# One attention phase: maxima taken in pairs, low parts of weight units one step behind, the convolution's split one group later

## The reference, cut to what matters

```python
proj = n @ w_in[l]
y_conv = short_conv_mixer(b_gate, c_gate, h_conv, conv_w[l], w_conv_out[l])
...
def short_conv_mixer(b_gate, c_gate, h_in, conv_w, w_out):
    u = c_gate * h_in
    up = jnp.pad(u, ((0, 0), (CONV_WIDTH - 1, 0), (0, 0)))
    conv = sum(up[:, k:k + S, :] * conv_w[k] for k in range(CONV_WIDTH))
    return (b_gate * conv) @ w_out
...
s = jnp.where(mask, s.astype(jnp.float32), -jnp.inf)
m = jnp.max(s, axis=-1, keepdims=True)
e = jnp.exp(s - m)
return e / jnp.maximum(jnp.sum(e, axis=-1, keepdims=True), 1e-30)
...
mix = jax.nn.sigmoid(g_conv) * y_conv + jax.nn.sigmoid(g_attn) * y_attn
h = h + mix @ w_o[l]
```

## Time and profile before

| | us |
|---|---|
| median of 3 runs | 761.01 (760.69 to 763.24) |
| the profiled execution | 764.64 |
| its span | 762.9 |
| TensorE busy | 752.9 |
| VectorE busy | 519.9 |
| ScalarE busy | 421.4 |

### The profile page before, as it was taken

The page is one execution under the profiler, slowest core; times in us unless marked ns, Lnnn a source line. Parts: engine busy times, 40 slices in busy tenths (PEclk is TensorE's granted clock), DMA queues, the critical chain, the costliest instruction groups (busy, mean ns, idle before and its releaser), DMA issues.

```text
span 762.9 us, 12541 instructions
## 1 busy us (share of the span) xinstructions
PE 752.9 (99%) x5015; PEld 668.0 (88%) x5015; DVE 519.9 (68%) x848; ACT 421.4 (55%) x808; POOL 71.0 (9%) x111
## 2 busy tenths in 40 slices
PE   9999999999999999999999999999999999999998
PEld 8999988798899988888888888999888888888886
DVE  4884676777574767888357766889568777447762
ACT  5484556457364447566345555697636665445640
POOL 6300000001011000250000003500100000000000
PEclk9999999999999999999999999999999999999999
DMA  7998454235334556665655562754453655655611
GB/s 238 307 310 276 77 124 141 99 111 166 111 112 172 172 181 194 196 214 187 218 181 192 169 217 59 231 157 141 163 166 122 210 200 188 218 168 170 210 63 56
DMA packets 108430, 131.33 MB, mean 172 GB/s; under 512 B 5357, under 2 KB 97595, under 8 KB 108372
## 3 DMA queue, kind: packets, MB, share of 16 engines
q1 hardware_dynamic: 105780, 125.58, 50.9%
q0 software_dynamic: 2304, 4.43, 2.6%
q10 hardware_dynamic: 288, 0.52, 0.2%
HBM read 128.68 MB, written 1.84 MB: 171 GB/s over the span
## 4 chain that ended last, share of the span: by engine, by line
PE 85%; DVE 9%; ACT 3%; issue 2%; DMA 0%; SPq 0%; ACTq 0%; DVEq 0%
PE B L1552 27%; PE B L1529 21%; PE B L1513 16%; PE B L1534 11%; DVE LO L978 3%; ACT PR L665 2%; PE B L1778 1%; DVE SM L1104 1%; PE B L1731 1%; PE B L1741 1%; PE B L1611 1%; PE B L1565 1%; DVE PR L1125 1%; PE B L1559 1%; DVE CG L1157 1%
## 5 line engine op out<-in xcount | busy, mean ns | idle before, releaser
L978 DVE TENSOR_TENSOR LO<-RAW,HI 128x1024 fp32r<-128x1024 f32 x236 | 281.8, 1230 | 109.3 <-ACT HI L539 108.8
L539 ACT ACTIVATE HI<-RAW 128x1024 fp32r<-128x1024 f32 (+1 forms) x240 | 237.1, 1037 | 58.0 <-PE B L1552 57.4
L1529 PE MATMUL B<-AA,HI 128*128 128x512 f32 x704 | 243.4, 398 | 0.5 <-DVE AA L984 0.5
L1552 PE MATMUL B<-HI,AA 128*128 128x512 f32 (+1 forms) x832 | 216.7, 346 | 0.1
L1534 PE MATMUL B<-AA,LO 128*128 128x256 f32 x704 | 183.2, 281 | 0.0
L1513 PE MATMUL B<-AA,HI 128*128 128x256 f32 x896 | 167.7, 288 | 3.0 <-DVE SGC L1180 1.9
L1552 PEld LDWEIGHTS B<-HI,AA 128*128 128x128 f32 x832 | 146.0, 189 | 20.1 <-issue 1.1
L1529 PEld LDWEIGHTS B<-AA,HI 128*128 128x128 f32 x704 | 126.7, 188 | 25.2 <-issue 1.1
L1513 PEld LDWEIGHTS B<-AA,HI 128*128 128x128 f32 x896 | 140.3, 192 | 7.5 <-issue 2.9
L1552 PE MATMUL B<-LO,AA 128*128 128x512 f32 (+1 forms) x416 | 143.2, 344 | 0.0
L1534 PEld LDWEIGHTS B<-AA,LO 128*128 128x128 f32 x704 | 132.9, 189 | 8.2
(11 more groups left out here) (308 smaller groups left out, 653.8 us busy)
## 6 DMA issues: line engine op xcount, KB each, us to landing
RAW<-in_w_in SPq DMA_DIRECT2D x29, 1024.0 KB, 6.0
RAW<-in_w_gate SPq DMA_DIRECT2D x22, 1024.0 KB, 5.1
RAW<-in_w_up SPq DMA_DIRECT2D x22, 1024.0 KB, 5.1
RAW<-in_w_down SPq DMA_DIRECT2D x22, 1024.0 KB, 4.9
RAW<-in_w_in SPq DMA_DIRECT2D x10, 512.0 KB, 6.2
RAW<-in_w_attn_out SPq DMA_DIRECT2D x4, 1024.0 KB, 5.3
RAW<-in_w_o SPq DMA_DIRECT2D x4, 1024.0 KB, 5.0
RAW<-in_w_out SPq DMA_DIRECT2D x4, 1024.0 KB, 5.0
```

The source lines that it names most:

```text
L539: e.activation(pieces(HI, NSPL, i, k), pieces(RAW, NRAW, i, k), ACT.Copy).then_inc(split_hi, 1)
L978: e.tensor_tensor(pieces(LO, NSPL, i, k), pieces(RAW, NRAW, i, k), pieces(HI, NSPL, i, k), ALU.subtract).then_inc(split_lo, 1)
L1529: return e.matmul(dst[:, :], hi[:, t, c0:c0 + 128], flatten(AA[:, ch + t, :, :]), start=(t == 0), stop=(t == nk - 1))
L1552: x = e.matmul(dst, a, w[:, t, c0:c0 + n], start=(first and t == 0 and k == 0), stop=(last and t == nk - 1 and k == 2))
```

## The change

On VectorE the low parts of weight units are taken out of the fill-in generator and put in one of their own (`splits`), in the same order. A step first takes the maxima of both members where a pair begins, and none in the second step of a pair; then the low parts that the step before would have taken; then the weights; then its fill-in. On VectorE and ScalarE the split of the convolution's result (`convolved`) is moved behind the next fill-in piece: the high and low part of channel 0 come with piece 9, channel 1 with piece 10, channel 2 with piece 15, channel 3 with piece 16. TensorE, GpSimd and SyncE keep their lists.

```diff
--- before.py
+++ after.py
@@ -691,6 +691,10 @@
                         e.activation(dst[:, ch, :], B[c][:, 0:S], ACT.Tanh, scale=0.5).then_inc(gate_tanh, 1)
                         yield
 
+            def convolved(n):
+                e.wait_ge(bg_sb, n + 1)
+                e.activation(AH[:, 8 + n, :], CG[:, n % 2, :], ACT.Copy).then_inc(conv_hi, 1)
+
             def fill():
                 u = U_FILL
                 hi(u + 2)
@@ -705,6 +709,8 @@
                     u = U_FILL + 2 + 3 * i
                     hi(u + 2)
                     for c in range(2):
+                        if i == 1 and c == 0:
+                            convolved(1)
                         e.wait_ge(cg_pe, 2 * i + c + 1)
                         if i == 1:
                             e.wait_ge(conv_lo, c + 1)
@@ -714,11 +720,11 @@
                     yield
                     yield
                     hi(u + 4)
-                    for c in range(2):
-                        e.wait_ge(bg_sb, 2 * i + c + 1)
-                        e.activation(AH[:, 8 + 2 * i + c, :], CG[:, c, :], ACT.Copy).then_inc(conv_hi, 1)
-                        yield
+                    yield
+                    convolved(2 * i)
+                    yield
                 u = U_FILL + 8
+                convolved(3)
                 e.wait_ge(block_lo, 1)
                 yield from gates(SGC, u, 0)
                 u = U_FILL + 12
@@ -1131,20 +1137,33 @@
                 e.tensor_tensor(AL[:, c:c + 4, d], OB[:, :].rearrange("p (c q) -> p c q", c=4), AH[:, c:c + 4, d],
                                 ALU.subtract).then_inc(turn_lo, 1)
 
+            def splits():
+
+                for u in (*range(U_FILL + 2, U_FILL + 14), U_FILL + 14, None, U_FILL + 15, None, *range(U_FILL + 16, U_FILL + 20)):
+                    if u is None:
+                        yield
+                    elif U_FILL + 14 <= u < U_FILL + 16:
+                        lo(u)
+                        yield
+                    else:
+                        for c in range(2):
+                            lo(u, c)
+                            yield
+
+            def convolved(n):
+                e.wait_ge(conv_hi, n + 1)
+                e.tensor_tensor(AL[:, 8 + n, :], CG[:, n % 2, :], AH[:, 8 + n, :], ALU.subtract).then_inc(conv_lo, 1)
+
             def fill():
-                u = U_FILL
+                for _ in range(4):
+                    yield
                 for i in range(2):
                     for c in range(2):
-                        lo(u + i + 2, c)
-                        yield
-                for i in range(2):
-                    u = U_FILL + 2 + 3 * i
-                    for c in range(2):
-                        lo(u + 2, c)
+                        if i == 1 and c == 0:
+                            convolved(1)
                         yield
                     for c in range(2):
                         n = 2 * i + c
-                        lo(u + 3, c)
                         e.wait_ge(up_pe, n + 1)
                         e.wait_ge(cg_sb, n + 1)
                         if n == 0:
@@ -1159,43 +1178,41 @@
                         yield
                     for c in range(2):
                         n = 2 * i + c
-                        lo(u + 4, c)
                         own.wait()
                         e.wait_ge(bg_pe, n + 1)
                         e.tensor_tensor(CG[:, c, :], B[c][:, 0:S], CG[:, c, :], ALU.mult).then_inc(bg_sb, 1)
-                        e.wait_ge(conv_hi, n + 1)
-                        e.tensor_tensor(AL[:, 8 + n, :], CG[:, c, :], AH[:, 8 + n, :], ALU.subtract).then_inc(conv_lo, 1)
+                        if c == 1:
+                            convolved(2 * i)
                         yield
-                u = U_FILL + 8
-                for i in range(4):
-                    for c in range(2):
-                        lo(u + i + 2, c)
-                        yield
-                u = U_FILL + 12
+                convolved(3)
+                for _ in range(8):
+                    yield
                 for ch in range(8):
-                    if ch % 4 < 2:
-                        lo(u + ch // 4 + 2, ch % 4)
                     e.wait_ge(co_pe, ch + 1)
                     e.wait_ge(gate_sb, ch + 1)
                     e.tensor_tensor(SGC[:, ch, :], B[ch % 2][:, 0:S], SGC[:, ch, :], ALU.mult).then_inc(co_sb, 1)
                     if ch % 2 == 1:
                         yield
-                u = U_FILL + 14
-                for i in range(4):
-                    for c in range(2):
-                        lo(u + i + 2, c)
-                        yield
-
-            filler = fill()
+                for _ in range(8):
+                    yield
+
+            splitter, filler = splits(), fill()
             for i in range(NSTEP + 2):
-                if i < NSTEP:
+                if i < NSTEP and i in begins:
                     most(i)
+                    if i + 1 < NSTEP and i + 1 not in begins:
+                        most(i + 1)
+                if i > 0:
+                    for _ in range(FILL_AT[i - 1]):
+                        next(splitter)
                 if i < NSTEP:
                     weights(i)
                 for _ in range(FILL_AT[i]):
                     next(filler)
                 if i - 2 in ends:
                     taken(ends.index(i - 2))
+            for _ in splitter:
+                pass
             for _ in filler:
                 pass
             for ch in range(8):
```

## The result

| | us |
|---|---|
| kernel before, median of 5 runs | 762.16 (760.69 to 763.29) |
| changed kernel, median of 5 runs | 757.7 (757.22 to 761.82) |
| ratio | 0.9955, 95% interval 0.9933 to 0.9977 |
| profiled execution, before and changed | 764.64 and 757.58 |
| span, before and changed | 762.9 and 755.8 |

A forecast was written before the change was run, and what follows sets the result against it. TensorE, busy 99% of the span, was taken to bound the kernel, with 6.7 us of its attention time gettable. Terms -3.1 + 0.5 + 0 gave -2.6 to -2.7 us: 758.3 us from 761.01, range 756.4 to 761.0.

The forecast's parts named there:

- A to D: TensorE's four stands in the attention (0.84, 0.53, 0.90, 0.89 us), waiting for VectorE; all predicted gone, -3.1 us.
- the walk: Step prices carried through steps 2 to 19, TensorE held to its measured groups; about 3.2 us gained at step 13.
- E: TensorE's stand at step 20, 2.04 us before; predicted to grow by 0.5 us, low parts being queued before the weights.
- The SyncE queue: Loads issued one step (some 5.7 us) later; claimed covered, with about 34 us of room against a 6.0 us landing.
- The clock: TensorE's granted clock at half behind step 20's stand; cost taken as 1.6 us in both kernels, so change 0.
- second rival: The clock does not fall behind step 20's stand: another 1.6 us faster, 756.7 us; chance 0.12.
- The sum: All terms for the whole kernel: -3.1 + 0.5 + 0 = -2.6 to -2.7 us, median 758.3 us, -0.35%.
- Rivals 4 to 6: 4: gain partly handed back, 759.9 us, 0.14; 5: TensorE waits for weights, 766.3, 0.04; 6: nothing, 761.0, 0.03.
- VectorE's waits for the exponentials: VectorE's stands for ScalarE in the attention steps, 1.58 and 1.09 us a step; predicted to nearly vanish.
- Part (b): Low parts one step later, between maxima and weights on VectorE; predicted to fill the stand almost exactly in single pair steps.
- (a): Both maxima of a pair at once on VectorE; the second predicted to cost only 0.61 us ahead of the first weights.

The follow-up runs named there:

- e3: Changed kernel with the low parts put back behind the weights of their own step: median 757.09 us, ratio 0.9940.
- e5: Changed kernel, but in step 20 VectorE gates channels 2 and 3 straight behind the maxima, then weights, then low parts: median 756.32 us, ratio 0.9917.
- e9: The changed kernel measured once more, with no further edit: 759.24 us, ratio 0.9971 against the kernel before.
- e2: Kernel before with only both maxima of a pair taken at once: median 756.65 us, ratio 0.9936.

## Why the prediction was right, point by point

- **A to D, -3.1 us.** Right. At step 13 TensorE had gained 3.33 us on its own start (152.14 - 146.17 - 2.64), where the walk gave about 3.2.
- **The walk itself.** Taken(1) was put at 139.3 to 139.9 us and ran from 136.60 + 2.64 = 139.24; gate product 2 at 143.5, ran at 143.37; the gating behind E at 195.68 less the 3.3 gained and the 2.64 of the start, 189.74, ran at 189.66. Only taken(0) was off, by 1.4 us, for a reason that I had ruled out (next point).
- **The SyncE queue, "covered".** The outcome was right, the ground was wrong. ScalarE stood 2.26 us for a load in step 6. ScalarE's timeline of the changed kernel, and the row of VectorE's that waited for what follows:

```profile
110.90 2.00 ACT L539 ACTIVATE HI<-RAW 128x1024 fp32r<-128x1024 f32 x2 [2.26 <-DMA RAW<-in_w_in]
```

```profile
113.91 0.69 DVE L1137 TENSOR_TENSOR AA<-B,AA 128x512 fp32r<-128x512 f32 x1 [1.33 <-ACT AA L682]
```

  I had set 34 us of room against the median landing of 6.0 us, and the median was the wrong row. The load that ScalarE waited for went out at 80.0 us, as soon as its slot was free, and landed at 110.9. The same load of the kernel before, which went out at 82.6, was as slow. DMA issues from 80 to 84 us, before and changed (count, KB, us to landing):

```profile
RAW<-in_w_in SPq DMA_DIRECT2D x1, 1024.0 KB, 30.8
```

```profile
RAW<-in_w_in SPq DMA_DIRECT2D x1, 1024.0 KB, 30.9
```

  In the kernel before it landed at 113.4, and ScalarE came to it only at 114.49. e3, with the low parts back in their old places, shows the same wait of 2.3 us, so it isn't the move of the low parts but ScalarE's being earlier that uncovers it. TensorE did not notice: taken(0) ended at 114.6, wanted at 116.14. The 3 us of room were 1.5.
- **E, +0.5 us.** Right in place, cause and size: 2.48 us against 2.04 by starts, and e5 removes it whole.
- **The clock, 0.** Wrong for the profiled execution (it fell in that of before, not in that of the changed kernel; my second rival, at 0.12), right for the kernels: about one run in two in both. Its size, which I put at 1.6 us, is 1.5: 24 matmuls at full clock take 2.97 us (190.13 to 193.10 in the changed kernel), not 2.88. The term was taken from one trace, in which it looked like a fixed part of the stand. I should have called it a chance of a half in both kernels; the forecast's sum would have been the same.
- **The sum.** -2.6 to -2.7 us forecast. The traces give -2.9 to -3.0 for the change. The two profiled executions are 7.1 us apart, 4.4 more than forecast: 2.6 for the start, 1.5 for the clock, 0.3 for the change. The medians of the first measurement are 4.5 us apart, since they rest on five runs each and a run carries its start (first scores between 71.89 and 75.42 us in the thirteen traces) and a clock fall of 1.5 us or not. The repetition, e9 against before, gave a ratio of 0.9971, 2.2 us, and the fastest runs are 3.5 us apart in the first measurement (760.69 and 757.22) and 2.0 in the repetition (760.00 and 757.99). The forecast of -0.35% lies between 0.9955 and 0.9971. That the median came within 0.6 us of 758.3 is in part luck: of the 3.6 us that I took off the profiled execution most were, as far as the traces tell, its late start and its fallen clock, which I had not told apart, and the median of before itself moved from 761.01 to 762.16 with two more runs.
- **Rivals 4 to 6.** None came: E is TensorE's only wait in the loop, so no stand came back and none on weights appeared. Two maxima in one go take 1.28 to 1.29 us, what two single ones at the old price take (0.61 and 0.68), so reading a second bank costs nothing that can be seen.
- **VectorE's waits for the exponentials "should nearly vanish".** Too strong: from 30.5 to 9.7 us. Eight times VectorE still comes to the weights before ScalarE has the exponentials; before the longest wait, 1.64 us up to 171.09, ScalarE itself stood 1.83 us for a projection whose gate it does ahead of the exponentials.
- **Part (b) as the main part.** The prediction priced the three parts in one walk and never each alone. That hid that (a) alone does A to D, and that (b) is what makes E grow: with (a) alone the same arithmetic (1.77 + 1.22 + 0.47 us behind the scores) would have given E 0.8 to 0.9 us and 1.6 us more gain; e2 measured 1.00 by starts.

## What to carry to other kernels

An engine's stands that feed a late chain can often be removed by either of two moves; try each alone, since the second may buy nothing and put work in front of something urgent. Before filling a gap on one engine with useful work, look at the one step in which another engine waits for what comes behind the gap: there a short idle wait is cheaper than two microseconds of work that nobody needs yet. And when runs differ in their start, compare kernels from the first instruction of the changed phase to the end of the span.

## What the runs showed of the hardware that I had not expected

- The granted clock fell to half for 3 to 4 us behind a stand of 2.0 to 2.5 us in 42 of 90 runs, at a cost of 1.5 us; in 12 of 12 behind one of 4.0 us and in none of 52 where no single stand was over 1.9 us. Two stands of 0.8 and 1.3 us with a projection between them never brought it, one of 2.0 us on the same chip did in 16 of 23. The Trainium skill, "TensorE: Matmul & The Clock Gate", Part 1, says of the start of a kernel that the monitor runs freely and that the number of slow matmuls therefore differs between runs of one kernel; the runs agree, at the start (26 matmuls in 3.17 and in 4.80 us in two executions of the changed kernel) and behind E.
- The pace of the start decides when the attention begins. The 26 matmuls took 3.17 us in eight of the thirteen traces, with the first scores at 71.89 to 72.54 us; 4.60 to 4.80 in three (73.35 to 74.09), and 5.82 and 5.83 in two (75.42 and 74.96). The granted clock doesn't tell them apart: in e9's trace the window from 6 to 9 us has 0.75 (the last but two of the numbers), while the trace of before shows 1.00 there and yet runs at about half the pace of the changed kernel's. The column and the pace don't agree in the first microseconds; that is left open.

```profile
6.00:9.00 3.00, 3.00 (x20) 2.64 (x18) 2.04 (x4) 1.62 (x5) 0.00 (x0) 0.75 1.07 366
```

- Loads of 1 MB that land in 5 to 6 us elsewhere took 30.8, 22.3 and 16.0 us in the kernel before when they went out at 82.6, 93.9 and 103.1 us. They share this stretch with a store of 768 KB that went out at 76.3 and took 35.1 us; the load that went out ahead of the store, at 72.3, took 5.4 us, and in both kernels the first slow load landed about 2 us behind the store. The median over all 29 loads, 6.0 us, shows nothing of it. That the store is the cause is likely and not shown: no run moved it.

```profile
bias_rows<-OH POOLq DMA_DIRECT2D x1, 768.0 KB, 35.1
```
